# Sliding attention: the values of four tiles at once on column halves of the array, and each pair's gates projected in its own steps

## The reference, cut to what matters

```
s = q @ k.T * 64**-0.5 - slope * dist          # only the last 128 keys of each query
m = max(rowmax(s), sink)
p = exp(s - m);  p = p / (sum(p) + exp(sink - m))
o_swa = p @ v                                   # 128 queries x 64, per head
o = concat([o_mla, o_swa]) * silu(gate)         # gate = h @ w_gate, 512 columns for o_swa
x = x + o @ w_out
```

## Time and profile before

| | us |
|---|---|
| median of three runs | 2779.51 |
| lowest, highest | 2777.7, 2782.37 |
| the profiled execution's own time | 2778.66 |
| its span in the profile | 2777.4 |
| PE busy in the span | 2612.2 (94%) |
| DVE busy | 951.7 (34%) |
| ACT busy | 597.3 (22%) |
| mean granted clock of TensorE | 0.968 of full speed |

### The profile page before, as it was taken

How to read it: one execution, slowest core, us unless ns; L and a number is a source line. 1 busy time by engine, 2 the same in 40 slices (tenths; PEclk the granted TensorE clock), 3 DMA queues, 4 the chain that set the end, 5 groups by cost and what they waited for, 6 DMA issues and landing times. The chain is left out here.

```text
span 2777.4 us, 28921 instructions
## 1 busy us (share of the span) xinstructions
PE 2612.2 (94%) x11550; PEld 1690.2 (61%) x11550; DVE 951.7 (34%) x2513; ACT 597.3 (22%) x1502; POOL 118.0 (4%) x140
## 2 busy tenths in 40 slices
PE   7899989999999999999989999999999999689992
PEld 4688766764466666656644467754464665477771
DVE  4344503442212222222332456663410134521115
ACT  3344313331122232222321111110000210011111
POOL 1000000000000000000000000000000000012212
PEclk9999999979999999999999999999999999789996
DMA  4000020031211110111041200004140122338876
GB/s 152 31 1 1 1 76 1 1 107 68 77 31 46 46 29 18 46 46 46 31 109 66 80 31 5 31 31 144 61 166 24 61 93 91 122 105 265 269 232 189
DMA packets 146955, 210.40 MB, mean 76 GB/s; under 512 B 17008, under 2 KB 101872, under 8 KB 146816
## 3 DMA queue, kind: packets, MB, share of 16 engines
q1 hardware_dynamic: 139904, 183.33, 20.2%
q0 software_dynamic: 6912, 25.17, 3.8%
HBM read 170.66 MB, written 37.81 MB: 75 GB/s over the span
## 5 line engine op out<-in xcount | busy, mean ns | idle before, releaser
L170 PE MATMUL banks<-arena 128*128 128x512 f32 (+15 forms) x9422 | 2408.5, 431 | 52.6 <-DVE arena L2774 8.3
L170 PEld LDWEIGHTS banks<-arena 128*128 128x128 f32 (+4 forms) x9422 | 1469.9, 190 | 865.7 <-issue 756.3
L173 PE MATMUL banks<-arena 128*128 128x128 f32 (+1 forms) x1936 | 297.5, 283 | 63.3 <-DVE arena L427 15.7
L173 PEld LDWEIGHTS banks<-arena 128*128 128x128 f32 (+1 forms) x1936 | 234.8, 146 | 137.0 <-issue 82.6
L252 POOL TENSOR_TENSOR arena<-arena 128x1 f32<-128x1 f32 (+1 forms) x88 | 56.7, 646 | 2374.2 <-DVE arena L1144 1459.9
L1481 DVE CUSTOM_DVE_ANT_0 arena<-arena,banks 128x256 f32<-128x256 f32 (+7 forms) x128 | 91.4, 751 | 190.3 <-PE banks L170 190.2
L1437 ACT ACTIVATE arena<-arena 128x256 f32<-128x256 f32 (+7 forms) x128 | 98.2, 768 | 105.3 <-DVE arena L1481 105.3
L1139 DVE TENSOR_TENSOR arena<-arena,banks 128x1024 f32<-128x1024 f32 x16 | 19.5, 1221 | 170.0 <-PE banks L170 170.0
L1113 ACT ACTIVATE arena<-banks 128x512 f32<-128x512 f32 x32 | 18.8, 588 | 266.0 <-PE banks L173 266.0
L1504 DVE COPY arena<-banks 128x128 f32<-128x128 f32 (+3 forms) x32 | 15.7, 491 | 174.9 <-PE banks L173 174.9
L663 ACT ACTIVATE arena<-banks,arena 128x128 f32<-128x128 f32 (+7 forms) x64 | 47.4, 740 | 111.0 <-DVE arena L688 110.7
(11 more groups left out here) (275 smaller groups left out, 1280.6 us busy)
## 6 DMA issues: line engine op xcount, KB each, us to landing
x_scratch<-arena SPq DMA_DIRECT2D x40, 512.0 KB, 2.7
arena<-in_o_w_in_dram SPq DMA_DIRECT2D x32, 512.0 KB, 6.7
arena<-x_scratch SPq DMA_DIRECT2D x32, 512.0 KB, 5.6
arena<-in_w_gate_dram SPq DMA_DIRECT2D x16, 1024.0 KB, 15.3
arena<-in_w_up_dram SPq DMA_DIRECT2D x16, 1024.0 KB, 17.5
arena<-in_w_down_dram SPq DMA_DIRECT2D x16, 1024.0 KB, 8.4
arena<-in_x_dram SPq DMA_DIRECT2D x16, 512.0 KB, 4.5
arena<-decay_scratch SPq DMA_DIRECT2D x16, 512.0 KB, 6.2
```

The costliest lines, as they stand in the source:

```text
L170: return pe.matmul(o, a, b, start=start, stop=stop)
L173: return pe.transpose(o, a, ident)
```

## The change

The values now come four tiles at a time (a group, two groups to a pair). The stationary operand is the 64 columns of values and the moving one the turned weights of 128 columns, so that the output is turned already: head 0 on partitions 0 to 63 of bank 6, head 1 on 64 to 127, the two heads' matmuls issued one after the other. For this the turned weights are kept for eight tiles instead of four (`PW`). DVE no longer multiplies the values but the gate of each tile by the reciprocal (L1052, 128x128, `sw_gr`); four such gates are turned together (bank 4 or 5), ACT copies the bank out (L1016, 128x512), and DVE multiplies bank 6 with the copy into `OT` (L1059, 128x512). The 32 single turns of gated tiles and the 32 copies behind them go.

The units are in another order. Ahead of the steps are 12 (keys, values, pair 0's queries). Step s holds the gate of its own tile s, and steps 2 and 5 of each of the first three pairs hold a query half of the next pair as well, behind the transposes. So the last pair's steps hold eight gates. The second half of the output weights is loaded after the last query half and not after the last unit.

```diff
         SW = [scr(20 + 2 * i, 512) for i in range(4)]
-        PW = [scr(28 + 2 * i, 512) for i in range(4)]
+        PW = [scr(28 + 2 * i, 512) for i in range(8)]
+        GRS = [tiled(scr(44, 512), 4), tiled(XB[2][:, 512:1024], 4)]
+        GRTS = scr(46, 512)
...
+        SWA_FIRST = [("k", 0, 0), ("k", 0, 1)] + [("v", 0, t) for t in range(8)] + [("q", 0, 0), ("q", 0, 1)]
+        SWA_STEPS = [[("g", s // 8, s % 8)] + ([("q", s // 8 + 1, s % 8 // 5)] if s < 24 and s % 8 in (2, 5) else []) for s in range(32)]
+        SWA_UNITS = SWA_FIRST + [u for step in SWA_STEPS for u in step]
...
+        def swa_queries(p):
+            return SWA_UNITS.index(("q", p, 1)) + 1
...
+        def pe_swa_unit(unit, b, free):
             P.wait_ge(f_a, swa_fa + free)
-            q, j = (u - 10) // 10, u % 10
-            if free > 10:
-                P.wait_ge(gate_done, swa_g + 8 * ((free - 10) // 10) + max((free - 10) % 10 - 2, 0))
-            if u < 2:
+            P.wait_ge(gate_done, swa_g + swa_gates(free))
...
-            for u in range(20):
-                pe_swa_filler(u, 6 + u % 2, u - 1)
+            for n, unit in enumerate(SWA_FIRST):
+                pe_swa_unit(unit, 6 + n % 2, n - 1)
...
                     P.wait_ge(sw_added, s - 1)
-                    P.wait_ge(f_a, swa_fa + 10 + 10 * p + 2)
+                    P.wait_ge(f_a, swa_fa + swa_queries(p))
                     for h in range(2):
                         m = mm(sc[:, 512 * h + lo:512 * h + 256], QS[p % 2][64 * h:64 * h + 64, 128 * t:128 * t + 128],
                                KS[p // 2][64 * h:64 * h + 64, k0:k0 + 256 - lo], True, True)
                     m.then_inc(ws_done.sem, 1)
-                    for u in swa_units(s)[:1]:
-                        pe_swa_filler(u, 7, u)
+                if s >= 5 and s % 4 == 1:
+
+                    g = s // 4 - 1
+                    p = g // 2
+                    P.wait_ge(sw_out, swa_turn["p", s - 2] + 1)
+                    P.wait_ge(sw_gated, g)
+                    for i in range(4 * g, 4 * g + 4):
+                        t = i % 8
+                        blocks = [1] if t == 0 else [0, 1]
+                        for c in blocks:
+                            for h in range(2):
+                                m = mm(bank(6)[64 * h:64 * h + 64, 128 * (i % 4):128 * (i % 4) + 128],
+                                       VS[:, t - 1 + c, 64 * (p // 2):64 * (p // 2) + 64],
+                                       PW[i % 8][:, 256 * h + 128 * c:256 * h + 128 * c + 128], c == blocks[0], c == 1)
+                    m.then_inc(sw_pv.sem, 1)
+                for unit in swa_steps(s)[:1]:
...
-                if 2 <= s <= 33:
-                    i = s - 2
-                    p, t = i // 8, i % 8
-                    blocks = [1] if t == 0 else [0, 1]
-                    P.wait_ge(sw_out, swa_turn["p", i] + 1)
-                    P.wait_ge(sw_gated, i)
-                    P.wait_ge(gate_done, swa_g + 8)
-                    for h in range(2):
-                        for c in blocks:
-                            m = mm(bank(6)[:, 64 * h:64 * h + 64], PW[i % 4][:, 256 * h + 128 * c:256 * h + 128 * c + 128],
-                                   VS[:, t - 1 + c, 64 * (p // 2):64 * (p // 2) + 64], c == blocks[0], c == 1)
-                    m.then_inc(sw_pv.sem, 1)
-                if s >= 3:
-                    i = s - 3
-                    k = swa_turn["o", i]
-                    P.wait_ge(sw_gated, i + 1)
+                for unit in swa_steps(s)[1:]:
+                    pe_swa_unit(unit, 7, SWA_UNITS.index(unit))
+                if s >= 6 and s % 4 == 2:
+                    g = s // 4 - 1
+                    k = swa_turn["o", g]
+                    P.wait_ge(sw_gr, 4 * g + 4)
                     P.wait_ge(sw_out, k - 1)
-                    tr(bank(4 + k % 2)[:, 0:128], OG[i % 2]).then_inc(sw_turned.sem, 1)
-                for u in swa_units(s)[1:]:
-                    pe_swa_filler(u, 7, u)
+                    for m_ in range(4):
+                        m = tr(bank(4 + k % 2)[:, 128 * m_:128 * m_ + 128], GRS[g % 2][:, m_, :])
+                    m.then_inc(sw_turned.sem, 1)
...
                     k = swa_turn["p", i]
                     C.wait_ge(sw_turned, k + 1)
-                    C.wait_ge(sw_pv, i - 3)
-                    act.activation(tiled(PW[i % 4], 2)[:, :, lo:256], tiled(bank(4 + k % 2), 2)[:, :, lo:256],
+                    C.wait_ge(sw_pv, i // 4 - 1)
+                    act.activation(tiled(PW[i % 8], 2)[:, :, lo:256], tiled(bank(4 + k % 2), 2)[:, :, lo:256],
                                    ACT.Copy).then_inc(sw_out.sem, 1)
-                if s >= 3:
-                    i = s - 3
-                    k = swa_turn["o", i]
+                for unit in swa_steps(s)[1:]:
+                    act_swa_unit(unit, 7)
+                if s >= 6 and s % 4 == 2:
+                    g = s // 4 - 1
+                    k = swa_turn["o", g]
                     C.wait_ge(sw_turned, k + 1)
-                    act.activation(OT[:, 4 + i // 8, 128 * (i % 8):128 * (i % 8) + 128], bank(4 + k % 2)[:, 0:128],
-                                   ACT.Copy).then_inc(sw_out.sem, 1)
-                for u in swa_units(s)[1:]:
-                    act_swa_filler(u, 7)
+                    C.wait_ge(sw_gated, g)
+                    act.activation(GRTS, bank(4 + k % 2), ACT.Copy).then_inc(sw_out.sem, 1)
...
+                if 2 <= s <= 33:
                     i = s - 2
-                    p, t = i // 8, i % 8
-                    a8 = at8[i % 6]
-                    V.wait_ge(sw_pv, i + 1)
-                    V.wait_ge(gate_done, swa_g + 8 * p + t + 1)
-                    if i >= 2:
-                        V.wait_ge(sw_turned, swa_turn["o", i - 2] + 1)
+                    p, t, a8 = i // 8, i % 8, at8[i % 6]
+                    V.wait_ge(gate_done, swa_g + i + 1)
+                    if i >= 8:
+                        V.wait_ge(sw_turned, swa_turn["o", i // 4 - 2] + 1)
                     vs.done()
-                    for h in range(2):
-                        m = vec.scalar_tensor_tensor(OG[i % 2][:, 64 * h:64 * h + 64], bank(6)[:, 64 * h:64 * h + 64],
-                                                     a8[:, 6 + h:7 + h], GT[p % 2][:, t, 64 * h:64 * h + 64], MUL, MUL)
-                    m.then_inc(sw_gated.sem, 1)
-                for u in swa_units(s)[1:]:
-                    dve_swa_filler(u, 7)
+                    vec.tensor_tensor(tiled(GRS[i // 4 % 2][:, i % 4, :], 2), tiled(GT[p % 2][:, t, :], 2),
+                                      a8[:, 6:8].rearrange("p (h c) -> p h c", c=1).to_broadcast([128, 2, 64]),
+                                      MUL).then_inc(sw_gr.sem, 1)
+                if s >= 7 and s % 4 == 3:
+                    g = s // 4 - 1
+                    V.wait_ge(sw_pv, g + 1)
+                    V.wait_ge(sw_out, swa_turn["o", g] + 1)
+                    vec.tensor_tensor(OT[:, 4 + g // 2, 512 * (g % 2):512 * (g % 2) + 512], bank(6), GRTS,
+                                      MUL).then_inc(sw_gated.sem, 1)
+                for unit in swa_steps(s):
+                    dve_swa_unit(unit, 7)
...
-            Y.wait_ge(f_pe, swa_f + 50)
+            Y.wait_ge(f_pe, swa_f + swa_queries(3))
```

More of the change, by code:

```diff
@@ L849, in program @@
         sw_turned, sw_out, sw_pv, sw_gated = event("window_turned"), event("window_turned_out"), event("window_values"), event("window_gated")
-        ws_done = event("window_scores")
-        for e in (sw_added, sw_max, sw_exp, sw_pv, sw_gated, ws_done):
+        ws_done, sw_gr = event("window_scores"), event("window_gates_by_sums")
+        for e in (sw_added, sw_max, sw_exp, ws_done, sw_gr):
             e.block(32)
-        sw_turned.block(64)
-        sw_out.block(64)
+        for e in (sw_pv, sw_gated):
+            e.block(8)
@@ L862, in pe_swa_filler, with swa_gates @@
+        SWA_UNITS = SWA_FIRST + [u for step in SWA_STEPS for u in step]
+        def swa_gates(n):
+            return len([u for u in SWA_UNITS[:max(n, 0)] if u[0] == "g"])
+        def swa_queries(p):
+            return SWA_UNITS.index(("q", p, 1)) + 1
+        def pe_swa_unit(unit, b, free):
             P.wait_ge(f_a, swa_fa + free)
-            q, j = (u - 10) // 10, u % 10
-            if free > 10:
-                P.wait_ge(gate_done, swa_g + 8 * ((free - 10) // 10) + max((free - 10) % 10 - 2, 0))
@@ L866, in pe_swa_filler @@
-            if u < 2:
+            P.wait_ge(gate_done, swa_g + swa_gates(free))
+            kind, q, j = unit
+            if kind == "k":
                 for k in range(NK):
-                    m = mm(bank(b), w_skv[:, k, 0:128], HT[:, k, 512 * u:512 * u + 512], k == 0, k == 7)
-            elif u < 10:
-                t = u - 2
+                    m = mm(bank(b), w_skv[:, k, 0:128], HT[:, k, 512 * j:512 * j + 512], k == 0, k == 7)
+            elif kind == "v":
                 for k in range(NK):
```

(22 more changed lines are left out.)

42 lines of the change are left out of this document (20 added, 22 removed).

## The result

The changed kernel takes 2767.37 us (median of five runs, 2762.43 to 2768.14) against 2779.59 us before (five runs, 2777.7 to 2782.37): a ratio of 0.995 with a 95% interval of 0.9939 to 0.9961, 12.2 us faster. The prediction was 2766.6 us, with a range of 2757 to 2777. The profiled execution has a span of 2766.0 us at a mean granted clock of 0.973.

The account below looks back on a forecast made before the run. TensorE was taken to bound pairs 0 to 2, with the VectorE and ScalarE loop nearly as slow. Terms -14.3 - 0.1 + 0.0 + 1.5 = -12.9 us gave 2766.6 us for the median, range 2757 to 2777.

Parts of the forecast that it names:

- Gates ahead of the steps, -14.3 us: Ahead of the sliding attention's steps: eight gate units of 1.79 us go, -14.3 us.
- +0.9 for the copy ahead of the first scores: Before pair 0's first scores, which now wait for the last query half's copy out: +0.9 us.
- A group in 1.95 us: Values of four tiles on column halves: eight slots, 1.85 us, taken as 1.95; before, four tiles take 3.36.
- Pairs 1 and 2 even, by 5.0 us of waits: Pairs 1 and 2: own work 3.6 us less, waits 5.0 us together, so 47.2 us against 47.29.
- Wait by wait: Pairs 1 and 2: query half behind L729 1.6, gate for bank 7 0.85, group for ScalarE's copy 0.7, step 5's gate 0.5.
- VectorE's product and its L1059 at nothing: VectorE's reciprocal product (0.29) and every fourth step's product (0.69): no cost while VectorE waits for ScalarE, 0.1 at most.
- Pair 0, 45.2: Pair 0: 44.3 us by the same walk plus 0.9 makes 45.2 against 45.31, -0.1 us.
- Last pair, 37.9 at full clock: Last pair with its gates: 31.7 us to the last scores' step's end plus a 6.2 tail, 37.9 against 36.41, +1.5.
- The projection's start at 0, between -2 and +3.5: Output projection's start: half-clock loss of 2.0 us left as is; -2 without a fall, +3.5 with a second stretch.
- The first rival: Whole stretch: TensorE alone decides, no new waits, -31.5 us, 2748 us; chance 0.10.
- The slower rival: Last pair: clock falls to half inside it and stays, +19 us there, sum +6, 2785 us; chance 0.07.
- The halves in turn: Groups of values: halves don't run together, eight groups at 3.5 instead of 1.95 us, +12.4, 2779 us; chance 0.04.

Follow-up runs that it names:

- order alone: Changed kernel's unit order (gates in their own pair's steps), but each tile's values by themselves as before, against the kernel before: 2765.3 us, ratio 0.9957.
- halves in turn: Changed kernel with each group's values matmuls reordered, all of head 0's first, then all of head 1's: 2776.5 us, ratio to before 0.9991.
- values alone: Kernel before with values of four tiles on column halves, projections kept in the order of before: 2773.9 us, ratio 0.9984.

## Why the prediction was right

Step by step, as the prediction had it:

- *Gates ahead of the steps, -14.3 us, and +0.9 for the copy ahead of the first scores.* The stretch of 14.38 us is gone; TensorE waits 0.69 us before the first scores. Right, and by the medians of "order alone" the whole gain.
- *A group in 1.95 us.* Right on average, by two errors that cancel. The prediction counts eight slots in every group, but the first of a pair has seven. A group of seven took 1.78 us and one of eight 2.00 (3.79 with its gate), 1.89 on average. The slots themselves take 0.218 us each ("halves in turn", last section), so that the way into the halves and back costs 0.25 us a group: near the 0.3 that was the upper bound for the drain which the Trainium skill names (TensorEngine Tiling (Array Packing), Tiling Modes), and not the 0.1 of the sum. The page gives no price for it.
- *Pairs 1 and 2 even, by 5.0 us of waits.* Measured 47.13 for 47.2 forecast. Wait by wait: 1.6 was 1.42, 0.85 was 0.79, 0.7 was 0.53, 0.5 was 0.35. These brackets count from the modelled end of the record before; from where the next matmul could have followed, the two waits of the query halves are 471.23 - 469.21 - 0.44 = 1.58 us and 491.39 - 490.44 - 0.44 = 0.51. The bank's part and the copy's part were shown by taking them away, -1.6 and -1.0 us a pair.
- *VectorE's product and its L1059 at nothing.* Doubling the product cost nothing. Right.
- *Pair 0, 45.2.* 44.72 from its first scores and the 0.8 ahead of them make 45.6. Right within half a microsecond.
- *Last pair, 37.9 at full clock.* 37.20, at 1.00. "Order alone" and "values alone" show that the clock stays because of the gates, as argued against the rival.
- *The projection's start at 0, between -2 and +3.5.* The term was mis-sized: it was -2.0, as the clock never fell. The tail is as thin as I said, but the clock was at full when it began and stayed there. Why it did, when it fell in the tail of "order alone", no run shows.

The forecast for the whole stretch was -12.9 us; it gave -15.7 in the profiled execution (10.7 of earlier start of the projection, 3.0 of late begin and 2.0 of clock). Elsewhere this execution lost the 3.0 us ahead and the 1.7 around 1400 us, which leaves about 11 us of the 11.4 between the spans. The medians differ by 12.2 us, 0.7 less than forecast. That the median came within 1 us of the forecast is therefore in part luck: a gain of 2.0 us that the sum held at nothing, 0.7 in the last pair, and the time lost elsewhere nearly cancel.

The first rival, 2748 us by TensorE's work alone, failed at the loop and at bank 7, as the Trainium skill's rule has it (TensorEngine Tiling (Array Packing), PSUM Bottleneck): the array got faster and the emptying of its banks then bound. The trace agrees, with 42.97 us busy in 47.13. But VectorE and ScalarE are busy only 21.55 and 16.91 us of it: it is not their throughput that binds, it is how long one bank, and the step's chain of operations, take to come free. With the query halves in bank 6 the time goes more than halfway to that rival, 2756.8. The slower rival, the clock inside the last pair, did not come. The halves in turn would have cost 9.9 us and not 12.4.

## What to carry to other kernels

Ask of each part of a change by itself which wait ends last where it acts: here the part that reads like a detail (which step projects which gates) is by the medians the whole gain, and the large rewrite of the values gives 1 us in the steps. Where several units share one accumulator bank, a saving on TensorE turns into waits for that bank; moving the query halves to a second bank, in the steps where it is idle, was worth 8 us, about 6 of them by the bank (steps of 174.2 and 168.0 us). It is the grouping of the values that leaves bank 6 idle in those steps. What the other places of the query halves would give without the grouping was not run. Work moved into a thin last stage counts twice: the last pair took eight more gates for 0.8 us more (37.20 for 36.41), as they kept the clock up.

## What the runs showed of the hardware

Matmuls on different column halves overlap even when they are not neighbours. In "halves in turn" the first group of a pair, without its gate, took 4.71 - 1.79 = 2.92 us for the 1.78 of the order by turns. Its single records in the trace show why it was not more: head 0's seven matmuls are fourteen records, 0.109 us apart but for the first, from 488.17 to 489.64 us, and head 1's first record stands at 489.32, when eleven of them had begun and three were to come. So head 1's matmuls started beside head 0's last ones, 0.43 us before they could have started behind them. In a group of sixteen matmuls, too, three of head 0's records were still to come.

A float32 matmul with 128 columns moving takes nearly the same with 128 columns of weights (0.223 us, 1.79 for eight) as with 64 (0.218), and one with 64 columns moving takes 0.21 (values of before, 0.84 us for four). From 128 moving columns down to 64 almost nothing is gained; turning the operands round cost nothing by itself, and the gain of the halves comes from the pairing.

TensorE at half clock does not come back by being busy alone: in before it had no idle time from 570.5 to 592.7 us and stayed at half, with transposes and matmuls of 64 columns. In "order alone" the same steps with gates of 128 columns stayed at full clock. With the values alone the clock of the last pair went to half three times (at 568.8, 579.1 and 592.7 us), each time in or behind waits of about 2 us (2.00, 2.18 and 2.17), and was back at full at 572.2, 585.9 and 599.5 us, each time within 1 us of the end of a group of values with its 128 columns moving (572.5, 586.0 and 598.5 us).
